# State-space decays by running sums with a matrix of ones, and ScalarE subtracting the column's sum per head

## What is computed

```python
    la = jnp.moveaxis((dt * a).reshape(bsz, nc, SSM_CHUNK, SSM_GROUPS, SSM_HEADS_PER_GROUP), 2, -1)
    cum = jnp.cumsum(la, axis=-1)
    ...
    causal = jnp.tril(jnp.ones((SSM_CHUNK, SSM_CHUNK), dtype=bool))
    decay = jnp.exp(jnp.where(causal, cum[..., :, None] - cum[..., None, :], -jnp.inf))
    cb = jnp.einsum("bclgn,bcsgn->bcgls", cm, bm)
    y_diag = jnp.einsum("bcgls,bcgels,bcsgep->bclgep", cb, decay, x)
    ...
    y_off = jnp.einsum("bclgn,bcgepn,bcgel->bclgep", cm, h_in, jnp.exp(cum))
    return (y_diag + y_off).reshape(bsz, seq, SSM_GROUPS, SSM_HEADS_PER_GROUP, SSM_HEADDIM)
```

## Time and profile before

| | |
|---|---|
| median of 3 runs | 2621.81 us |
| profiled execution | 2622.3 us |
| its span | 2620.1 us |
| PE busy | 2581.9 us (99%) |
| VectorE busy | 1735.3 us (66%) |
| ScalarE busy | 1402.0 us (54%) |
| GpSimd busy | 64.7 us (2%) |
| decay sums, L2067, PE x32 | 592 ns each, 15.0 us in all |
| product with ones, L2035, PE x16 | 591 ns each, 7.5 us in all |
| decay exponentials, L834, ScalarE x16 | 596 ns each, 8.7 us in all |
| exponentials of `cum`, L850, ScalarE x8 | 596 ns each, 4.3 us in all |

### The profile page before, as it was taken

How to read it: one execution, slowest core, us unless ns; L and a number is a source line. 1 busy time by engine, 2 the same in 40 slices (tenths; PEclk the granted TensorE clock), 3 DMA queues, 4 the chain that set the end, 5 groups by cost and what they waited for, 6 DMA issues and landing times.

```text
span 2620.1 us, 39067 instructions
## 1 busy us (share of the span) xinstructions
PE 2581.9 (99%) x14818; PEld 2245.3 (86%) x14818; DVE 1735.3 (66%) x2350; ACT 1402.0 (54%) x1918; POOL 64.7 (2%) x50
## 2 busy tenths in 40 slices
PE   7999999999999999999999999899999999999998
PEld 7999898888888888888888888788888888888887
DVE  5789976567755775576655666755577647764775
ACT  5588765456644554455544544654565535543554
POOL 2001210000000000000000000000000000000001
PEclk9999999999999999999999999999999999999999
DMA  6554344565555555555766566115655555555555
GB/s 222 163 178 145 129 137 150 188 201 192 184 193 189 188 192 193 193 185 173 212 197 203 165 187 186 61 50 192 212 189 192 191 193 184 187 192 193 193 172 165
DMA packets 238963, 465.67 MB, mean 178 GB/s; under 512 B 12558, under 2 KB 14206, under 8 KB 238718
## 3 DMA queue, kind: packets, MB, share of 16 engines
q1 hardware_dynamic: 237358, 461.77, 54.3%
q10 hardware_dynamic: 1488, 2.29, 0.3%
HBM read 461.94 MB, written 2.10 MB: 177 GB/s over the span
## 4 chain that ended last, share of the span: by engine, by line
PE 95%; ACT 2%; DVE 2%; DMA 1%; issue 1%; SPq 0%; ACTq 0%; DVEq 0%
PE bank L1811 33%; PE bank L1814 16%; PE bank L1848 10%; PE bank L1849 10%; PE bank L1850 10%; PE bank L2131 3%; PE bank L2132 3%; PE bank L2133 3%; PE bank L2239 1%; PE bank L2277 1%; ACT weight_head L656 1%; PE bank L2176 1%; PE bank L2067 1%; DMA weight_raw<-in_ab_w_in 1%; PE bank L2261 0%
## 5 line engine op out<-in xcount | busy, mean ns | idle before, releaser
L1155 DVE TENSOR_TENSOR weight_tail<-weight_raw,weight_head 128x2048 fp32r<-128x2048 f32 (+1 forms) x456 | 998.1, 2189 | 791.8 <-ACT weight_head L656 790.6
L656 ACT ACTIVATE weight_head<-weight_raw 128x2048 fp32r<-128x2048 f32 (+1 forms) x456 | 832.2, 1826 | 909.3 <-DMA weight_raw<-in_ffn_w_up 317.8
L1811 PE MATMUL bank<-norm_in,weight_head 128*128 128x512 f32 x3712 | 1167.1, 396 | 0.0
L1814 PEld LDWEIGHTS bank<-norm_in,weight_tail 128*128 128x128 f32 x3712 | 697.3, 188 | 164.7
L1814 PE MATMUL bank<-norm_in,weight_tail 128*128 128x256 f32 x3712 | 729.3, 278 | 0.0
L1811 PEld LDWEIGHTS bank<-norm_in,weight_head 128*128 128x128 f32 x3712 | 565.7, 189 | 1.3 <-issue 0.2
L1848 PE MATMUL bank<-weight_head,mixed 128*128 128x512 f32 x1088 | 425.9, 391 | 5.3 <-ACT zx L902 3.8
L1849 PE MATMUL bank<-weight_tail,mixed 128*128 128x512 f32 x1088 | 424.4, 390 | 0.0
L1850 PE MATMUL bank<-weight_head,mixed 128*128 128x512 f32 x1088 | 424.4, 390 | 0.0
L2131 PE MATMUL bank<-norm_in,weight_head 128*128 128x256 f32 x896 | 258.9, 289 | 2.6 <-DVE conf_pad L1413 1.1
L2132 PE MATMUL bank<-norm_in,weight_head 128*128 128x256 f32 x896 | 253.7, 283 | 0.0
(11 more groups left out here) (301 smaller groups left out, 1588.3 us busy)
## 6 DMA issues: line engine op xcount, KB each, us to landing
weight_raw<-in_ffn_w_up SPq DMA_DIRECT2D x176, 1024.0 KB, 5.0
weight_raw<-in_ffn_w_down SPq DMA_DIRECT2D x64, 1024.0 KB, 5.1
weight_raw<-in_cd_w_in SPq DMA_DIRECT2D x64, 1024.0 KB, 5.7
weight_raw<-in_ab_w_in SPq DMA_DIRECT2D x56, 1024.0 KB, 5.1
weight_raw<-in_ab_w_out SPq DMA_DIRECT2D x32, 768.0 KB, 4.3
weight_raw<-in_ffn_w_down SPq DMA_DIRECT2D x32, 768.0 KB, 4.4
weight_raw<-in_cd_w_out SPq DMA_DIRECT2D x32, 768.0 KB, 4.4
residual<-in_x SPq DMA_DIRECT2D x4, 512.0 KB, 5.7
```

Source lines behind the costliest of these rows:

```text
L656: act.activation(WHEAD[:, off % RING, 0:kt * CW], WRAW[:, off % RING, 0:kt * CW], ACT.Copy)\
L1155: dve.tensor_tensor(WTAIL[:, off % RING, 0:kt * CW], WRAW[:, off % RING, 0:kt * CW], WHEAD[:, off % RING, 0:kt * CW].bitcast(F32), ALU.sub ...
L1811: pe.matmul(bank[c][:, :], head, rhs[:, u * s.kt + k, :], start=u == 0 and k == 0, stop=False)
L1814: mm = pe.matmul(bank[c][:, 0:SEQ], tail, rhs[:, u * s.kt + k, 0:SEQ], start=False, stop=u == s.units - 1 and k == s.kt - 1)
```

## The change

The decay sums of both chunks are now the running sums themselves: ones times `LATS`, into banks 4 and 5. The product with ones after unit 2 goes. The sums by partition, one column a head and chunk, come from one small product (triangle times `la`, 64 columns) in group q = 4, copied by ScalarE into `CUM`. Per head, ScalarE takes `Relu(CUM - sum)` from the bank (eight operations of 128 columns), which is the negated difference clamped at zero, and then one exponential over all eight heads with scale -1, in place. The exponentials of `cum` for chunk 1 read the same banks 4 and 5, between the Relus and the large exponential. The waits follow.

```diff
@@ la_triangle (GpSimd)
-                if g and t == 0:
+                if g:
                     pool.wait_ge(d_done, m - 1)
-                if g and t == 1:
-                    pool.wait_ge(e_done, g)
@@ decay_exps (ScalarE)
                 act.wait_ge(d_done, m + 1)
+                act.wait_ge(cum_ready, 1)
                 if g:
                     act.wait_ge(ssd_y, m - 1)
-                for h in range(2):
-                    act.activation(DEC[t][:, 2 * h:2 * h + 2, :], bank[4 + h][:, :].rearrange("p (a b) -> p a b", a=2),
-                                   ACT.Exp).then_inc(exp_d, 1)
+                for h in range(HPG):
+                    c = 32 * t + HPG * g + h
+                    act.activation(DEC[t][:, h // 2, h % 2 * P:(h % 2 + 1) * P], bank[4 + h // 4][:, h % 4 * P:(h % 4 + 1) * P],
+                                   ACT.Relu, bias=CUM[:, c:c + 1], scale=-1.0).then_inc(d_read, 1)
+                if t == 1:
+                    c_exps(g)
+                act.wait_ge(d_read, HPG * (m + 1))
+                act.activation(DEC[t], DEC[t], ACT.Exp, scale=-1.0).then_inc(exp_d, 1)
@@ c_exps (ScalarE)
-                act.wait_ge(e_done, g + 1)
+                act.wait_ge(d_done, 2 * g + 2)
...
-                    act.activation(CE[:, h * 512:(h + 1) * 512], bank[6 + h][:, :], ACT.Exp).then_inc(exp_e, 1)
+                    act.activation(CE[:, h * 512:(h + 1) * 512], bank[4 + h][:, :], ACT.Exp).then_inc(exp_e, 1)
@@ ScalarE's turn: q == 5, and behind the fourth head split
+                    act.wait_ge(cum_sum, 1)
+                    act.activation(CUM, bank[6][:, HEADS:HEADS + NT * HEADS], ACT.Copy).then_inc(cum_ready, 1)
...
-                if ssd:
-                    c_exps(g)
@@ decay_masked (VectorE)
-                dve.wait_ge(exp_d, 2 * m + 2)
+                dve.wait_ge(exp_d, m + 1)
@@ between (PE)
+                    pe.matmul(bank[6][:, HEADS:HEADS + NT * HEADS], TRI[:, :], LA[:, 0:NT * HEADS], start=True, stop=True)\
+                      .then_inc(cum_sum, 1)
...
-                    pe.wait_ge(exp_d, 4 * g + 2)
+                    pe.wait_ge(d_read, HPG * (2 * g + 1))
                     decays(2 * g + 1)
                 if 0 <= g < GROUPS and u == 2:
-                    pe.wait_ge(cbm_ready, g + 1)
-                    pe.wait_ge(st_ready, g + 1)
-                    if g == 3:
-                        pe.wait_ge(ynorm_var, 1)
-                    for h in range(2):
-                        mm = pe.matmul(bank[6 + h][:, :], ONES[:, :], LATS[1][:, h * 512:(h + 1) * 512], start=True, stop=True)
-                    mm.then_inc(e_done, 1)
-                    pe.wait_ge(exp_d, 4 * g + 4)
+                    pe.wait_ge(d_read, HPG * (2 * g + 2))
+                    pe.wait_ge(exp_e, 2 * g + 2)
                     chunk_y(2 * g)
@@ decays (PE)
-                    mm = pe.matmul(bank[4 + h][:, :], UST[:, :], LATS[m % 2][:, h * 512:(h + 1) * 512], start=True, stop=True)
+                    mm = pe.matmul(bank[4 + h][:, :], ONES[:, :], LATS[m % 2][:, h * 512:(h + 1) * 512], start=True, stop=True)
```

More of the change, by code:

```diff
@@ L325, in build @@
         DALL = SMALL[:, 112:144]
+        CUM = S1
         POSI = at("pos_i", places["small"] + 4 * 384, [P, SEQ], I32)
@@ L376, in build @@
             "la_ready", "dte_sum", "dte_ready", "xd2_ready", "st_done", "st_ready"))
-        lat_ready, d_done, e_done, cb_done, cbm_ready, exp_d, exp_e, ce_ready, m_ready, ssd_y, y_read = (
-            sem(n) for n in ("lat_ready", "d_done", "e_done", "cb_done", "cbm_ready", "exp_d", "exp_e",
+        lat_ready, d_done, cb_done, cbm_ready, exp_d, exp_e, ce_ready, m_ready, ssd_y, y_read = (
+            sem(n) for n in ("lat_ready", "d_done", "cb_done", "cbm_ready", "exp_d", "exp_e",
                              "ce_ready", "m_ready", "ssd_y", "y_read"))
@@ L398, in build @@
         conf_halved, ysq_halved = sem("conf_halved"), sem("ysq_halved")
+        cum_sum, cum_ready, d_read = sem("cum_sum"), sem("cum_ready"), sem("d_read")
         vc_cleared, prob_cleared = sem("vc_cleared"), sem("prob_cleared")
@@ L2005, in between @@
                     pe.wait_ge(dte_ready, 1)
+                    pe.wait_ge(cum_ready, 1)
                     if g:
-                        pe.wait_ge(exp_e, 2 * g)
+                        pe.wait_ge(cbm_ready, g)
+                        pe.wait_ge(st_ready, g)
                     pe.wait_ge(btok_ready, g + 1)
@@ L2044, in between @@
                     else:
-                        pe.wait_ge(exp_e, 2 * g + 2)
+                        pe.wait_ge(st_ready, g + 1)
                     pe.transpose(bank[7][:, 0:P], BC[:, g + 1, 0:P], IDENT[:, :]).then_inc(bt_turned, 1)
                 if (q, u) == (11, 3):
-                    pe.wait_ge(exp_e, 2 * GROUPS)
+                    pe.wait_ge(cbm_ready, GROUPS)
                     group_spread(0)
@@ L2094, in group_sum @@
                 if g:
-                    pe.wait_ge(exp_e, 2 * GROUPS)
+                    pe.wait_ge(st_ready, GROUPS)
                 if g > 1:
```

## The result

The changed kernel takes 2642.31 us (median of 4 runs, 2639.63 to 2644.46), beside 2621.43 for the kernel before on the same chip: a ratio of 1.0076, 95% interval 1.0060 to 1.0092. The direction and the range held; the time is 7 us above the forecast, and above the forecast's own range of 2631 to 2637. The profiled execution, the slowest of the four, took 2644.46 us, with a span of 2642.2, 22.1 longer than before.

What follows compares the result with a forecast made beforehand. TensorE was taken to bound the kernel. Group losses of 3.0, 3.5 and 6.2 us plus 0.2 for the new product made 12.9, so 2621.8 + 13 = 2635 us; range 2626 to 2646, the forecast's own 2631 to 2637.

Steps and rivals of the forecast that it cites:

- TensorE bounds, and its waits are the price: Whole kernel: TensorE is busy 99% of the span, so what it sheds or waits for counts one for one.
- The product for the running sums, 0.2 us: The new 64-column product on TensorE: between 0.1 and 0.9 us, taken as 0.2.
- The Relus 0.25 us apart: ScalarE's eight Relus of a chunk: 0.25 us each, 2.12 us until the last has ended.
- The table load, 1.28 us behind the Relus: ScalarE's table load, formerly ahead of the first exponential, now follows the Relus; 1.28 us in the fourth group's sum.
- First group 3.0: First group slower by 3.0 us: TensorE waits of 2.75 and 2.0 before the two chunks' outputs, less 1.81 removed.
- Second and third 1.75 each: Second and third groups: TensorE waits 1.55, then 2.0 us, making each group 1.75 us slower.
- Fourth group 6.2: Fourth group: 3.1 us waiting for the squares plus 3.1 passed on through split and bank copies, 6.2 us slower.
- Behind the fourth group, no difference: After the fourth group all three engines are late by the same amount, with no slack on TensorE to absorb it.
- the waits cost clock as well: Rival: TensorE's clock falls behind long waits, 3.4 us a fall; one fall 2638, three 2645; chance 0.23.
- the rival of Relus without overlap: Rival on ScalarE: Relus 0.37 us apart make the change 20.6 us slower, 2642; no separate chance given.
- The reason that a slower TensorE shortens its next wait: Argument against clock loss: a slower TensorE gives ScalarE and VectorE time, which shortens its next wait; no size given.
- ScalarE has the room: Rival: the added 4.3 us fits ScalarE's 7.4 idle of 34, giving 7.0 us faster, 2615; faster given 0.07.

Runs made afterwards that it cites:

- e7: Change kept in the second chunk only, first chunk's decays as in the kernel before, next-weights split and first squares moved earlier on ScalarE: 2616.82 us, ratio 0.9978.
- e12: Second profile of the changed kernel with the first squares of the gated norm ahead of the fourth group's first decays on ScalarE: 2636.47 us, one run.
- e8: Kernel before, without the change, with the next-weights split and the first squares moved earlier on ScalarE: 2621.16 us, ratio 0.9996.
- e9: Kernel before with three more wide exponentials on ScalarE ahead of the fourth group's first ones, results written over: 2626.21 us, ratio 1.0011.
- e4: Kernel before with five more wide exponentials on ScalarE ahead of the fourth group's first ones, results written over: 2629.08 us, ratio 1.0027.
- e3: Changed kernel with the first squares of the gated norm moved ahead of the fourth group's first decays on ScalarE: 2636.32 us, ratio 1.0055.
- e2: Changed kernel with the next-weights split moved ahead of the convolution's four products on ScalarE in the four groups: 2635.43 us, ratio 1.0044.
- e5: Changed kernel with split and first squares moved earlier on ScalarE, in the fourth group the split also ahead of the second chunk's decays: 2626.22 us, ratio 1.0013.

## Why the prediction was right, and where it was short

- *TensorE bounds, and its waits are the price:* held. The chain is 91% TensorE, and e7 shows the 7.2 us of the removed product as a gain as soon as hardly anything waits (7.0 of busy time, 6.0 of the time).
- *The product for the running sums, 0.2 us:* it took 0.22.
- *The Relus 0.25 us apart:* eight of 0.38 us each fill 2.15, so (2.15 - 0.38) / 7 = 0.25. The Trainium skill's rule that the prediction weighed ("ScalarE: Activation LUTs", "What ACT_TABLE_LOAD costs") gave 0.29 as an estimate; this trace does not bear that out, and the row of the attention was the better guide.
- *The table load, 1.28 us behind the Relus:* it starts where the eighth Relu ends, at 236.92 in the first group, and takes 1.28. That it costs TensorE as much was not tested by itself.
- *First group 3.0:* 3.09, but made otherwise. The wait for the first chunk's output is the forecast one (2.74 for 2.7); the clock then fell, and the second wait was 0.53 in place of 2.0. In e12, the changed kernel but for the squares, the clock did not fall there, and the second wait is the forecast 1.96.
- *Second and third 1.75 each:* 1.82 and 1.82, with the waits of 1.47 and 1.96 that were named (1.55 and 2.0).
- *Fourth group 6.2:* 10.9. This is the term that failed. The wait for the squares was right (3.03 for 3.1), and the one at the bank copies too (3.62 for 3.8); but behind the first TensorE ran at 0.50 from 340 to 348 us, with the decays in twice their time, and ScalarE, which waited for those decays, passed the delay on. That is 4.7 us more (9.67 less 4.98), all that the term lacked.
- *Behind the fourth group, no difference:* 3.6 us. Up to the output product it is 2.73, and the clock of 0.61 and 0.54 from 368 to 376 accounts for it (0.39 x 2.46 + 0.46 x 4 = 2.8). The other 0.9 are 1.17 less and 2.06 more in work that the change does not touch. The first goes with a smaller fall behind the output product (0.86 and 0.71 from 424 to 432, where the kernel before had 0.50 and 0.67 from 404 to 412); of the second, 1.5 are waits ahead of products of the second layer (L1817), and e8, without the change, waits 1.0 there.

So the mechanism stood as forecast, and every wait but the first group's second; the loss of clock, some 7.5 us in two places, was set down as a rival at 0.23 ("the waits cost clock as well", 2638 to 2646) instead of as a term. The measured time lies inside the range because the range takes in that rival, so the forecast's own sum was short by it. That the rival of Relus without overlap gave 2642 too is chance: the rows have them 0.25 us apart, not 0.37. The reason given against the rival of the clock, that two of the waits were shorter than the one of 3.84 us in the trace before, is what the runs refuted: e9's wait of 1.4 us was followed by a fall, and e4 prices the clock behind one of 2.7 at 4.1 us by the medians, 3.3 by its trace. e3 took out the wait for the squares with its fall, and 5.5 us by the two ratios, in spite of a new fall in its second group. The reason that a slower TensorE shortens its next wait was right for one of the three falls of this trace alone, that in the first group.

"ScalarE has the room" failed for the reason the prediction gave: no busy share, but the list between its two blocks decides. e2 and e5 turned the order of that list and won some 8 and 16 us without taking any work off ScalarE.

## What to carry to other kernels

When work is moved to an engine with idle time, ask what is queued behind it there and who waits for that: the same operations cost 20 us in one order, 3 in another, and won 6 once only the half that freed TensorE's product was changed. A new wait on a busy TensorE is priced at its length and, where the clock falls behind it, at some microseconds more: in these traces 1.5 to 4.7 us, and nothing where the slower work ran into another wait.

## What was not expected of the hardware

- The clock's fall behind a wait is not the same from one execution to the next: 0.57 and 1.00 behind the same wait of 1.96 us, 0.79 and 1.00 behind the same one of 2.74. At the sum of squares, sixteen products of one column, it came in every profile with a wait there: 1.45, 1.46, 2.0, 2.7, 3.0 (twice) and 4.6 us. Whether the narrow products make it so was not tested.
- A fall is not always paid: ahead of another wait it cost nothing (the first group, 36.8 us long with it and without; the bank copies in e12), at the sum of squares 4.7 us. The room is limited: in e5 the clock of the first group was lower for longer than in e2 (0.50 in place of 0.68 from 240 to 244, 0.86 in place of 1.00 from 244 to 248), and the group took 37.46 us in place of 36.35.
